# The value rows of a hybrid decoder's attention made as channel rows and then transposed

## The chip, the cores and the metric

The kernel runs on one core of one Trainium2 chip. The metric is the device time of one execution in microseconds; the median of three runs stands for a kernel. The profiler takes one execution apart into instructions. Five engines work side by side and meet only at semaphores: TensorE (PE; its weight loads are listed apart as PEld), VectorE (DVE), ScalarE (ACT), GpSimd (POOL) and SyncE (SP), which issues the large transfers.

## What is computed

One inference step of two layers for 280 token rows: 272 prompt rows (16 of them learned meta tokens) and 8 sample rows. All arrays are float32. The part that matters here is the input projection of layer 0 and the attention that uses the value rows:

```python
def mixer_inputs(h, w_in, q_norm, k_norm, pos):
    z = h @ w_in
    u, q, k, v, qi, ki, wi = jnp.split(z, SPLITS, axis=-1)
    ...
    v = v.reshape(B, L, N_HEADS, HEAD_DIM)

def sparse_attend(q, kg, vg, valid):
    ...
    p = jax.nn.softmax(logits, axis=-1)
    out = jnp.einsum('bhqk,bqkhd->bqhd', p.astype(vg.dtype), vg, ...)
```

Here `h` is the normed input (280 rows of 1024), and `v` is 280 rows of 8 heads x 64 = 512. `v` is also an output of the step. Beside it layer 0 has a state-space part (`u`, a GELU and a gate called glu), an index score that selects 64 keys for each query, and a dense feed-forward part; layer 1 has a pooling mixer and a top-2-of-8 expert part.

## The kernel before

Constants: `T = 280` token rows, split into `TC = 3` chunks of 128, 128 and 24 (`TCN`), `C = 8` input chunks of 128 channels, `H = 8` heads of `HD = 64`. Activations lie channel-major: channels on the partitions, tokens along the free axis (`h3[:, c, t]`). Weights come in as units of 2 MB (`MIXER_UNITS`: u, qi, kw, q, k, v, glu, wout0, wout1) into three slots.

**PSUM.** TensorE writes into eight banks of 128 x 512. `fill_order()` (L151) lists every fill of layer 0 up to the expert part in the order in which TensorE makes them. The seven banks of `BANKS` are dealt out by turns along that list, and a fill has to wait until the fill before it in its bank is released: `open_fill` waits for that, `filled` waits for a fill, `emptied` for its release. So the list sets both the order on TensorE and who waits for whom.

**The projections.** q, k, qi and kw are made by `channels` (L899): a block of 128 weight columns is stationary, the 280 tokens move, 8 matmuls of 128x280 for each of 4 blocks. The result is channel-major. The value rows are made the other way round, by `project` (L879): 128 (or 24) tokens of `h3` are stationary and 512 weight columns move, so that the result is token-major, as the attention needs it (`z3["v"]`, keys on the partitions).

**The order around the value rows on TensorE.** After the index dots (L1021) and the last state output come `value_rows(0)` and `value_rows(1)` (L1034, L1035), 8 matmuls of 128x512 each, then the four glu fills (L1042), which wait for the GELU (semaphore `gelu`, made by POOL at L811). Then the attention's own list: `logits(0)` and `logits(1)` (L1103, one matmul a head), `kself` (L1074), `("qB", b)` for samples 0 to 4 (L1084, L1085), `value_rows(2)` (8 matmuls with 24 tokens stationary), the transposed probabilities `pT` (L1111), `("att", 0)` (L1122), `logits(2)`, the key rows `kt` (12 transposes, L1097), `attT` (L856), qB 5 and 6, `pT` of chunk 1, qB 7, `att` 1, and so on to `satt` (L1137), the sample's attention over the cached values, and then the output projection.

**ScalarE** copies the value rows out of PSUM (`copy_rows`, recorded at L1466) between the steps of the GELU, takes the tanh of the glu fills (L1581) and makes the gate (L1583), then the exponentials (`exps`, L1591), and behind them the copies of v 2, `pT`, `kt`.

**VectorE** runs the top-64 selection (L2050, L2054) and turns it into a mask (L2059, L2060); then `mask_logits(0)` (L2066), the gate product (L2091), `mask_logits(1)`, five `key_logits(b)` (L2105 product, L2108 sum over the head, one pair for each sample), `scale_rows(0)` (L2084, which waits for `("att", 0)`), `mask_logits(2)`, `key_logits` 5 to 7 and `scale_rows(1)`.

**SP** loads the v unit into slot 2. The next unit in that slot, wout1 (L590), waits for the last fill that reads v, by `last_fill` (L145).

Of the kernel before, what the change touches and what calls it, by code (L numbers as in the profile page):

```python
# [24 lines left out]
P = 128  # L25
D = 1024
C = D // P
NP_ = 272
NB = 8
T = NP_ + NB  # L30
TC = 3
TCN = [128, 128, 24]
# [112 lines left out]
def last_fill(unit):  # L145

    if unit == "v":
        return (unit, TC - 1)
    if unit in ("u", "qi", "q", "k", "glu"):
        return (unit, 3)  # L150
    if unit.startswith("wout"):  # L151
        return ("wout", 4 * int(unit[4:]) + 3)
    if unit.startswith("ffn"):
        return ("up", 2 * int(unit[3:]) + 1)
    if unit.startswith("down"):
        return ("down", int(unit[4:]))
    return ("pool", C - 1) if unit == "pool" else unit
# [12 lines left out]
def fill_order():  # L170
# [14 lines left out]
    f += index_order()  # L185
    f += [("v", 0), ("v", 1)] + [("glu", c) for c in range(4)]
    def logits(t):
        return [("logit", t, h) for h in range(H)]
# [4 lines left out]
    def spread(*bs):  # L193
        return [("qB", b) for b in bs]

    f += logits(0) + logits(1) + ["kself"] + spread(0, 1, 2, 3, 4) + [("v", 2)] + probs_T(0) + [("att", 0)] + logits(2)
    f += [("kt", t) for t in range(TC)] + [("attT", 0)] + spread(5, 6) + probs_T(1) + spread(7) + [("att", 1)]
# [21 lines left out]
FILLS = fill_order()  # L219
FILL_NO = {name: n for n, name in enumerate(FILLS)}  # L220
SAMPLE_BANK = 7

# [4 lines left out]
def bank_of(name):  # L227
    return SAMPLE_BANK if name in SAMPLE_FILLS else FILL_NO[name] % BANKS


def bank_uses(name):

    if name in SAMPLE_FILLS:
        return SAMPLE_FILLS.index(name) + 1
    return FILL_NO[name] // BANKS + 1

# [8 lines left out]
PASS_FILL_AT = {name: k for names in PASS_FILLS for k, name in enumerate(names)}  # L245
BEFORE_FILL = [sum(bank_of(n) == b for n in FILLS) for b in range(BANKS)] + [len(SAMPLE_FILLS)]

# [45 lines left out]
def hybrid_step(nc, a, o):  # L293

    with ExitStack() as ctx:
# [116 lines left out]
        kself = qbd[:, 1408:1408 + 64]  # L412
        sqh = zk[:, 0:4 * T].rearrange("p (c t) -> p c t", c=4)
        kisT = zv[:, 0:2 * PAST].rearrange("p (r k) -> p r k", r=2)
        srelu = zv[:, 2 * PAST:2 * PAST + SK]
# [415 lines left out]
        def _(pe):  # L831
# [46 lines left out]

            def project(name, width, t, out):  # L879

                w = unit(name, width)
                for c in range(C):
                    last = mm(out[0:TCN[t], 0:width], h3[:, c, t * P:t * P + TCN[t]], w[:, c, :],  # L883
                              start=(c == 0), stop=(c == C - 1))
                return last

            def state_inputs(j):
# [140 lines left out]

            def value_rows(t):

                unit_there("v")
                project("v", 512, t, open_fill(("v", t))).then_inc(full(("v", t)), 1)

            value_rows(0)  # L1034
            value_rows(1)  # L1035
            unit_there("glu")
# [32 lines left out]
            for name in [n for n in FILLS if n[0] in PROMPT_FILLS or n in PROMPT_FILLS]:  # L1069
# [17 lines left out]
                nq = QN[t]  # L1087
                if name == ("pT", 0, 0):
                    value_rows(2)
                if name == ("att", 2):  # L1090
# [354 lines left out]
        def _(act):  # L1445
# [128 lines left out]
            A(gb, ga, ACT.Identity, scale=0.044715, bias=ones[:, 0:1]).then_inc(sem("gelu_factor"), 1)  # L1574
            copy_rows(("v", 0), z3["v"])
            act.wait_ge(sem("gelu_arg"), 1)
            A(gb, ga, ACT.Tanh, scale=GELU_C).then_inc(sem("gelu_tanh"), 1)
            copy_rows(("v", 1), z3["v"])
            for c in range(4):
# [29 lines left out]
            exps(1, 4, H)  # L1609
            copy_rows(("v", 2), z3["v"])  # L1610
            copy_probs(0, 0)
# [913 lines left out]
```

## Time and profile before

| What | us |
|---|---|
| median of three runs (1565.76, 1572.68, 1574.19) | 1572.68 |
| the profiled execution: span from its first to its last instruction | 1572.0 |
| TensorE busy | 1526.3 (97%) |
| VectorE busy | 1297.4 (83%) |
| ScalarE busy | 992.9 (63%) |
| the expert part, from about 560 to the end | some 1010 |

The profiled execution's own time is its span of 1572.0 us; it stands 0.7 us under the median of the runs, and what lies around the span is not listed apart. The page cuts the span into 40 equal slices of 39.3 us; the work of this change lies in the fifth to seventh:

```profile
PE   6998899999998999999999999999999999999998
DVE  8978883666644899899889889889989889988886
ACT  5111342544432677777787787777777778777774
PEclk9999798999999899999999999999999999999999
```

Each digit is the busy share of a slice in tenths; PEclk is the clock that TensorE was granted, in tenths of full speed.

### The profile page before, as it was taken

The page shows a single profiled execution, that of the slowest core. Times are in us where ns is not written, and L with a number is a line of the kernel's source. Part 1 is how long each engine was busy: PE and PEld are TensorE (multiplying, and loading weights), DVE is VectorE, ACT ScalarE, POOL GpSimd, SP SyncE. Part 2 cuts the span into 40 slices and gives each one's busy share as a digit, 9 for nine tenths or more (in the row PEclk, how much of TensorE's full clock was granted, in tenths as well). Part 3 has the DMA queues.
Part 4 walks back from the last instruction along what each step waited for, and adds up shares of the span by engine and source line. Part 5 has one row for each costly group of instructions (what it writes and reads, how often), then busy time and mean ns, then how long its engine had stood idle before and what let it go on. Part 6 is the DMA issues. An engine that isn't in the chain of part 4 may idle for free.

```text
span 1572.0 us, 23245 instructions
## 1 busy us (share of the span) xinstructions
PE 1526.3 (97%) x7600; PEld 1228.8 (78%) x7600; DVE 1297.4 (83%) x1721; ACT 992.9 (63%) x1304; POOL 109.1 (7%) x155
## 2 busy tenths in 40 slices
PE   6998899999998999999999999999999999999998
PEld 5665465999998678888888888888888888888886
DVE  8978883666644899899889889889989889988886
ACT  5111342544432677777787787777777778777774
POOL 1277600000000000000000000000000000000000
PEclk9999798999999899999999999999999999999999
DMA  6401144454464479999989989999999999999992
GB/s 232 161 28 54 60 164 134 154 181 161 128 180 157 155 287 367 360 318 354 383 309 358 370 317 361 365 337 330 371 346 324 371 353 316 368 372 327 347 363 86
DMA packets 212890, 420.82 MB, mean 268 GB/s; under 512 B 10233, under 2 KB 56469, under 8 KB 212572
## 3 DMA queue, kind: packets, MB, share of 16 engines
q1 hardware_dynamic: 211542, 414.37, 74.1%
q10 hardware_dynamic: 622, 3.45, 0.6%
q0 software_dynamic: 672, 2.32, 0.4%
q8 instruction: 29, 0.48, 0.1%
q14 instruction: 25, 0.20, 0.0%
HBM read 417.50 MB, written 3.07 MB: 268 GB/s over the span
## 4 chain that ended last, share of the span: by engine, by line
PE 84%; DVE 3%; issue 1%; ACT 1%; SPq 0%; DMA 0%; ACTq 0%; DVEq 0%
PE bank L1352 20%; PE bank L1351 20%; PE bank L1347 20%; PE bank L1186 3%; PE bank L1190 3%; PE bank L1189 3%; PE bank L1372 2%; PE bank L1201 1%; PE bank L1205 1%; PE bank L1204 1%; PE bank L883 1%; PE bank L1307 1%; PE bank L1387 1%; PE bank L1153 1%; PE bank L1156 1%
## 5 line engine op out<-in xcount | busy, mean ns | idle before, releaser
L2266 DVE TENSOR_TENSOR split<-raw_w,split 128x1024 fp32r<-128x1024 f32 x672 | 787.2, 1218 | 36.6 <-ACT split L1736 32.7
L1736 ACT ACTIVATE split<-raw_w 128x1024 fp32r<-128x1024 f32 x672 | 688.6, 1060 | 119.0 <-PE bank L1347 117.1
L1347 PE MATMUL bank<-split,xgr 128*128 128x512 f32 x896 | 357.5, 399 | 1.1 <-DVE xgr L2333 1.1
L1352 PE MATMUL bank<-split,xgr 128*128 128x512 f32 x896 | 353.5, 395 | 0.0
L1351 PE MATMUL bank<-split,xgr 128*128 128x512 f32 x896 | 353.3, 394 | 0.0
L1352 PEld LDWEIGHTS bank<-split,xgr 128*128 128x128 f32 x896 | 168.7, 188 | 39.5
L1347 PEld LDWEIGHTS bank<-split,xgr 128*128 128x128 f32 x896 | 168.8, 188 | 38.6 <-issue 1.3
L1351 PEld LDWEIGHTS bank<-split,xgr 128*128 128x128 f32 x896 | 168.9, 188 | 37.6
L1347 PE MATMUL bank<-split,hbr 128*128 128x512 f32 x448 | 178.0, 397 | 0.0
L1352 PE MATMUL bank<-split,hbr 128*128 128x512 f32 x448 | 176.9, 395 | 0.0
L1351 PE MATMUL bank<-split,hbr 128*128 128x512 f32 x448 | 176.8, 395 | 0.0
L1186 PE MATMUL bank<-split 128*128 128x280 f32 x352 | 102.8, 292 | 0.0
L1190 PE MATMUL bank<-split 128*128 128x280 f32 x352 | 102.5, 291 | 0.0
L1189 PE MATMUL bank<-split 128*128 128x280 f32 x352 | 102.1, 290 | 0.0
L1352 PEld LDWEIGHTS bank<-split,hbr 128*128 128x128 f32 x448 | 84.3, 188 | 19.8
L1347 PEld LDWEIGHTS bank<-split,hbr 128*128 128x128 f32 x448 | 84.3, 188 | 19.2
L1351 PEld LDWEIGHTS bank<-split,hbr 128*128 128x128 f32 x448 | 84.4, 188 | 19.1
L1685 ACT ACTIVATE split<-ring 128x1024 fp32r<-128x1024 f32 x44 | 46.6, 1059 | 65.2 <-PE bank L1186 65.2
L1818 ACT ACTIVATE late<-bank 128x512 f32<-128x512 f32 x56 | 33.5, 598 | 71.8 <-PE bank L1352 71.8
L2376 DVE TENSOR_TENSOR hbr<-bank,hbr 128x512 fp32r<-128x512 f32 x56 | 38.6, 689 | 48.4 <-ACT hbr L1795 48.2
L2176 DVE TENSOR_TENSOR split<-ring,split 128x1024 fp32r<-128x1024 f32 x44 | 53.9, 1225 | 19.2 <-ACT split L1685 19.1
L1186 PEld LDWEIGHTS bank<-split 128*128 128x128 f32 x352 | 66.3, 188 | 0.0
(433 smaller groups left out, 1976.3 us busy)
## 6 DMA issues: line engine op xcount, KB each, us to landing
raw_w<-in_moe_gate SPq DMA_DIRECT2D x112, 1024.0 KB, 5.7
raw_w<-in_moe_up SPq DMA_DIRECT2D x112, 1024.0 KB, 6.1
raw_w<-in_moe_down SPq DMA_DIRECT2D x112, 1024.0 KB, 5.9
ring<-in_w_gate SPq DMA_DIRECT2D x11, 1024.0 KB, 5.1
ring<-in_w_up SPq DMA_DIRECT2D x11, 1024.0 KB, 7.4
ring<-in_w_down SPq DMA_DIRECT2D x8, 1408.0 KB, 6.6
ring<-in_w_in SPq DMA_DIRECT2D x5, 2048.0 KB, 9.7
ring<-in_w_out SPq DMA_DIRECT2D x2, 2048.0 KB, 8.1
```

The lines of the kernel that those rows point to most:

```text
L1186: first = mm(out[:, 0:T], w[0][:, c, :], dense_in(0, c), start=(c == 0), stop=False)
L1189: mm(out[:, 0:T], w[0][:, c, :], dense_in(1, c), start=False, stop=False)
L1190: last = mm(out[:, 0:T], w[1][:, c, :], dense_in(0, c), start=False, stop=(c == C - 1))
L1347: first = mm(out, hi, place[:, s, 0, cols], start=start, stop=False)
L1351: mm(out, lo, place[:, s, 0, cols], start=False, stop=False)
L1352: last = mm(out, hi, place[:, s, 1, cols], start=False, stop=stop)
L1685: A(place[:, n % FF_PLACES, 0, :].rearrange("p (c m) -> p c m", c=C), unit(name, 256)[:, k * C:(k + 1) * C, (f % 2) * P:(f % 2) * P + P], ...
L1736: A(place[:, s, 0, :], raw_w[:, at:at + BLOCK], ACT.Copy).then_inc(sem("high_ready"), 1)
L1818: A(th[:, j % 2, :], bank[b][:, :], ACT.Silu).then_inc(bank_free[b], 1)
L2176: TT(low_, unit(f"ffn{f // 2}", 256)[:, k * C:(k + 1) * C, (f % 2) * P:(f % 2) * P + P], high.bitcast(F32), ALU.subtract).then_inc(sem("ff ...
L2266: TT(place[:, s, 1, :], raw_w[:, at:at + BLOCK], place[:, s, 0, :].bitcast(F32), ALU.subtract).then_inc(sem("low_ready"), 1)
L2376: TT(dst, src, high.bitcast(F32), ALU.subtract).then_inc(bank_free[PASS_BANK[name]], 1)
```

## The change

The value rows are now made in two steps. First `channels` makes four channel-major fills `("vc", 0..3)` out of the v unit, as it does for q and k: a block of 128 weight columns is stationary and the 280 tokens move. ScalarE copies each to `vT3`, a part of `za` that is free by then. Then TensorE transposes them into token rows, 4 blocks for each of the 3 chunks, and ScalarE copies these to `z3["v"]` as before. All three chunks are made ahead of glu; `value_rows(2)` behind qB 4 is gone. The list gets three `skip` entries, which take a number but no bank use, so that banks are now looked up in a table `FILL_AT`.

```diff
@@ def last_fill(unit):
     if unit == "v":
-        return (unit, TC - 1)
+        return ("vc", 3)
@@ def fill_order():
-    f += [("v", 0), ("v", 1)] + [("glu", c) for c in range(4)]
+    f += four("vc") + [("skip", k) for k in range(3)] + [("v", t) for t in range(TC)] + four("glu")
...
-    f += logits(0) + logits(1) + ["kself"] + spread(0, 1, 2, 3, 4) + [("v", 2)] + probs_T(0) + [("att", 0)] + logits(2)
+    f += logits(0) + logits(1) + ["kself"] + spread(0, 1, 2, 3, 4) + probs_T(0) + [("att", 0)] + logits(2)
@@
+def fill_table():
+
+    used, table = [0] * BANKS, {}
+    for n, name in enumerate(FILLS):
+        if name[0] != "skip":
+            used[n % BANKS] += 1
+            table[name] = (n % BANKS, used[n % BANKS])
+    return table
@@ hybrid_step
+        vT3 = za[:, 1, :, :]
@@ tensor
-            def project(name, width, t, out):
-
-                w = unit(name, width)
-                for c in range(C):
-                    last = mm(out[0:TCN[t], 0:width], h3[:, c, t * P:t * P + TCN[t]], w[:, c, :],
-                              start=(c == 0), stop=(c == C - 1))
-                return last
...
-            value_rows(0)
-            value_rows(1)
+            for c in range(4):
+                channels(("vc", c), "v", c * P, P)
+            for t in range(TC):
+                out = open_fill(("v", t))
+                for c in range(4):
+                    if t == 0:
+                        emptied(pe, ("vc", c))
+                    last = nc.tensor.transpose(out[0:TCN[t], c * P:(c + 1) * P], vT3[:, c, t * P:t * P + TCN[t]], ident)
+                last.then_inc(full(("v", t)), 1)
...
-                if name == ("pT", 0, 0):
-                    value_rows(2)
@@ scalar
-            copy_rows(("v", 0), z3["v"])
+            copy_channels(0)
             act.wait_ge(sem("gelu_arg"), 1)
             A(gb, ga, ACT.Tanh, scale=GELU_C).then_inc(sem("gelu_tanh"), 1)
-            copy_rows(("v", 1), z3["v"])
+            for c in range(1, 4):
+                copy_channels(c)
+            for t in range(TC):
+                copy_rows(("v", t), z3["v"])
...
             exps(1, 4, H)
-            copy_rows(("v", 2), z3["v"])
             copy_probs(0, 0)
```

On TensorE, behind the last index dots, before (L883 is `project`, L1042 the glu fills, L1103 the logits):

```order
L1021 MATMUL bank<-ring,low 16x272 x8
L883 MATMUL bank<-ring,hT 128x512 x16
L1042 MATMUL bank<-ring 128x280 x16
L1103 MATMUL bank<-low 128x128 x8
L1103 MATMUL bank<-low 128x256 x8
```

and at the same place in the changed kernel (line numbers are the changed file's: L910 is `channels`, L1042 the new transposes, L1050 glu, L1109 the logits):

```order
L1027 MATMUL bank<-ring,low 16x272 x8
L910 MATMUL bank<-hT,ring 128x280 x32
L1042 MATMUL bank<-consts,low 128x128 x8
L1042 MATMUL bank<-consts,low 24x128 x4
L1050 MATMUL bank<-ring 128x280 x16
L1109 MATMUL bank<-low 128x128 x8
L1109 MATMUL bank<-low 128x256 x8
```

The 16 matmuls of 512 columns became 32 of 280 and 12 transposes, all ahead of glu.

Further on, on TensorE, from the last qB fill (qB 4) to `("att", 0)`, before:

```order
L1084 MATMUL bank<-qsr 128x512 [waits bank1_free]
L1085 MATMUL bank<-qsr 128x512
L883 MATMUL bank<-ring,hT 24x512 [waits bank2_free,slot2_full]
L883 MATMUL bank<-ring,hT 24x512 x7
L1111 MATMUL bank<-consts,ring 128x128 [waits probs,bank3_free]
```

and now, down to the fourth logits fill of chunk 2 (L1092 and L1093 are qB 4, L1117 `pT`, L1128 `att` 0, L1109 the logits):

```order
L1092 MATMUL bank<-qsr 128x512 [waits bank2_free]
L1093 MATMUL bank<-qsr 128x512
L1117 MATMUL bank<-consts,ring 128x128 [waits probs,bank3_free]
L1117 MATMUL bank<-consts,ring 128x128 x3
L1117 MATMUL bank<-consts,ring 128x128 [waits probs,bank4_free]
L1117 MATMUL bank<-consts,ring 128x128 x3
L1128 MATMUL bank<-low,ring 128x64 [waits bank3_free,bank4_free,bank2_free,bank5_free]
L1128 MATMUL bank<-low,ring 128x64 x7
L1109 MATMUL bank<-low 16x272 [waits bank6_free]
L1109 MATMUL bank<-low 16x272 [waits bank0_free]
L1109 MATMUL bank<-low 16x272 [waits bank1_free]
L1109 MATMUL bank<-low 16x272 [waits bank2_free]
```

The 8 matmuls with 24 tokens stationary are gone. qB 4 lies in bank 2 now, the bank that the fourth logits fill of chunk 2 takes next; before, that bank held v 2, and the third logits fill took the bank of qB 4.

## Rows read from the trace of the kernel before

**Rows 1.** The page: span, and the chain that ended last by engine

```profile
span 1572.0 us, 23245 instructions
...
PE 84%; DVE 3%; issue 1%; ACT 1%; SPq 0%; DMA 0%; ACTq 0%; DVEq 0%
```

**Rows 2.** The chain in order of time, 176 to 268: start us, us, what

```profile
178.79 13.93 PE bank L883 x32
192.72 1.59 issue
194.31 7.79 PE bank L1042 x32
...
209.37 0.43 PE bank L1084
...
211.93 8.62 PE bank L883 x16
...
248.47 3.62 PE bank L1137 x4
...
263.86 1.93 PE bank L1137 x4
```

**Rows 3.** The timeline, 191 to 203: start us, us, engine, line, operation [idle before <-releaser]

```profile
191.66 2.55 POOL L811 TENSOR_TENSOR ring<-ring 128x1120 f32<-128x1120 f32 x1
...
201.71 0.43 DVE L2060 SCALAR_TENSOR_TENSOR ring<-ring,consts 40x272 f32<-40x272 f32 x1
...
202.13 0.40 ACT L1581 ACTIVATE ring<-bank 128x280 f32<-128x280 f32 x1 [1.48 <-PE bank L1042]
...
202.67 0.29 DVE L2066 CUSTOM_DVE_ANT_0 ring<-bank,ring 128x128 f32<-128x128 f32 x1 [0.53 <-PE bank L1103]
```

**Rows 4.** The timeline, 221 to 229: `scale_rows(0)` (L2084) and what follows

```profile
221.32 1.22 DVE L2108 TENSOR_REDUCE low<-low 128x16 f32<-128x1024 f32 x1
...
224.46 0.69 DVE L2084 TENSOR_TENSOR ring<-bank,small 128x512 f32<-128x512 f32 x1 [1.81 <-PE bank L1122]
...
226.22 1.53 PE L1097 MATMUL bank<-consts,low 128*128 128x128 f32 x12
...
227.59 0.60 PE L856 MATMUL bank<-consts,ring 128*128 128x128 f32 x4
...
228.88 1.22 DVE L2105 TENSOR_TENSOR low<-ring,bank 128x1024 f32<-128x1024 f32 x1 [0.49 <-PE bank L1085]
```

**Rows 5.** TensorE in stretches: window us, length, busy (x), granted clock, DMA share, GB/s

```profile
164.00:174.00 10.00, 10.00 (x37) 0.50 0.00 1
...
190.00:196.00 6.00, 4.41 (x14) 1.00 0.04 11
...
206.00:208.00 2.00, 1.40 (x11) 1.00 0.00 0
...
209.00:214.00 5.00, 5.00 (x10) 0.50 0.01 2
...
215.00:216.00 1.00, 1.00 (x3) 0.92 0.53 158
...
220.00:236.00 16.00, 14.80 (x112) 1.00 0.88 294
...
240.00:252.00 12.00, 11.68 (x61) 0.50 0.08 22
...
562.00:1572.00 1010.00, 1003.96 (x4480) 1.00 0.94 340
```

**Rows 6.** The chain, 150 to 300: four transposes (of the sample's query rows) at the half clock

```profile
169.67 0.94 PE bank L1015 x4
```

**Rows 7.** The timeline, 229 to 248: chunk 1's `pT` and `att`, chunk 2's exponentials, `att` 2

```profile
229.24 1.97 PE L1111 MATMUL bank<-consts,ring 128*128 128x128 f32 x16
...
231.85 0.51 ACT L1591 ACTIVATE ring<-ring,small 16x272 f32<-16x272 f32 x1
...
232.14 3.76 PE L1122 MATMUL bank<-low,ring 128*128 128x64 f32 x32 [0.27 <-ACT ring L1466]
...
236.13 1.34 PE L1111 MATMUL bank<-consts,ring 16*128 16x16 f32 x24 [0.24 <-ACT ring L1591]
...
237.08 0.69 DVE L2084 TENSOR_TENSOR ring<-bank,small 128x512 f32<-128x512 f32 x1
...
240.09 6.95 PE L1122 MATMUL bank<-low,ring 128*16 128x64 f32 x48
```

More of the change, by code:

```diff
@@ L220 @@
 FILL_NO = {name: n for n, name in enumerate(FILLS)}
+def fill_table():
[5 more added lines that the diff above has]
+    return table
+FILL_AT = fill_table()
 SAMPLE_BANK = 7
@@ L227, in bank_of @@
 def bank_of(name):
-    return SAMPLE_BANK if name in SAMPLE_FILLS else FILL_NO[name] % BANKS
+    return SAMPLE_BANK if name in SAMPLE_FILLS else FILL_AT[name][0]
 def bank_uses(name):
@@ L234, in bank_uses @@
         return SAMPLE_FILLS.index(name) + 1
-    return FILL_NO[name] // BANKS + 1
+    return FILL_AT[name][1]
 PASS_FILLS = [[("gate", j) for j in range(0, FC, 2)], [("up", j) for j in range(0, FC, 2)],
@@ L245 @@
 PASS_FILL_AT = {name: k for names in PASS_FILLS for k, name in enumerate(names)}
-BEFORE_FILL = [sum(bank_of(n) == b for n in FILLS) for b in range(BANKS)] + [len(SAMPLE_FILLS)]
+BEFORE_FILL = [sum(bank_of(n) == b for n in FILL_AT) for b in range(BANKS)] + [len(SAMPLE_FILLS)]
 AHEAD_FILLS = {PASS_BANK[name]: k for name, k in ((("gather", 0), 2), (("gather", 1), 2), (("y", 0), 1), (("y", 1), 1))}
@@ L1027, in _ @@
                        start=True, stop=True).then_inc(full("sscore"), 1)
-            def value_rows(t):
-                unit_there("v")
-                project("v", 512, t, open_fill(("v", t))).then_inc(full(("v", t)), 1)
-            value_rows(0)
-            value_rows(1)
+            for c in range(4):
[7 more added lines that the diff above has]
+                last.then_inc(full(("v", t)), 1)
             unit_there("glu")
@@ L1574, in _, with copy_channels @@
             A(gb, ga, ACT.Identity, scale=0.044715, bias=ones[:, 0:1]).then_inc(sem("gelu_factor"), 1)
-            copy_rows(("v", 0), z3["v"])
+            def copy_channels(c):
+                filled(act, ("vc", c))
+                copy_out(("vc", c), vT3[:, c, :], n=T)
+            copy_channels(0)
             act.wait_ge(sem("gelu_arg"), 1)
             A(gb, ga, ACT.Tanh, scale=GELU_C).then_inc(sem("gelu_tanh"), 1)
-            copy_rows(("v", 1), z3["v"])
+            for c in range(1, 4):
+                copy_channels(c)
+            for t in range(TC):
+                copy_rows(("v", t), z3["v"])
             for c in range(4):
```

## The prediction

> **What bounds the kernel.** I read the page first. TensorE holds 84% of the chain that ended last, VectorE 3% [rows 1]. Then TensorE in stretches: from 562 us to the end it is busy for 1003.96 of 1010 us at the full clock [rows 5], so nothing that happens in the mixer changes that part; it can only shift it. The question is by how much the hand-over to the output projection, near 266 us, comes earlier or later. There the chain in order of time names the value rows: 13.93 us for chunks 0 and 1, a gap of 1.59, glu for 7.79, and 8.62 for chunk 2 [rows 2]. That looks like 22.55 us of work on the path. The timeline of the other engines says that most of it is not. VectorE runs its selection until 202.14 and takes up the first logits at 202.67, with 0.53 us idle [rows 3]: TensorE and VectorE arrive there within half a microsecond of each other. And while TensorE makes the value rows of chunk 2, VectorE is in its key products and sums until 222.54 and then waits 1.81 us for `att` 0 [rows 4]. So the second piece has cover for all but 1.81 us, and the first has a partner that is just as late.
>
> **Part 1, the value rows ahead of glu.** The trace records a float32 matmul twice, so 16 matmuls of 512 columns are 32 records. Glu is 32 records with 280 columns and 128 stationary columns, in 7.79 us: 0.243 us each [rows 2]. The new fills have the same form: 4 fills x 8 matmuls x 2 records x 0.243 = 15.6 us, from 178.79 to 194.4. Bounds: by columns alone, from the 512-column record (13.93 / 32 = 0.435, x 280 / 512 = 0.238), 15.2; from above, by the 24-token matmuls, which began at the half clock (8.62 / 16 = 0.54 a record [rows 2], x 280 / 512 = 0.295), 18.9. I take glu's, the same form at the clock that holds there. Then the last block must be copied by ScalarE before its transpose: some 0.1 to hand over, 0.40 for a copy of 128x280 [rows 3], 0.1 back: 195.0. Of the 12 transposes three need only earlier copies; the other nine go at the pace of the key rows' transposes, 12 in 1.53, or 0.12 each with what follows [rows 4], 1.1 us: 196.1. Glu's other condition, the GELU, is ready at 194.21 [rows 3], so the gap of 1.59 is filled, not added. Glu ends at 203.9 instead of 202.10: **+1.8 us**, and VectorE, which had only 0.53 of its own wait there, begins the logits 1.8 later. ScalarE's extra work (4 copies of 0.40 and one more of rows) lies under TensorE's 15.6 us, except the last copy, counted above. Its wait for the fourth block stands behind the tanh of the GELU, so it holds back nobody but the glu tanh, which comes later anyway. SP's load of wout1 is released by the vc fills, ahead of the place where SP is; POOL issues its third store of value rows some 20 us sooner, and nobody waits for it until the stores are asked for behind the output projection's start.
>
> The rows give 0.12 us from one transpose to the next. The Trainium skill, page "TensorE: Matmul & The Clock Gate", Part 4 on the PE-mode transpose, gives about 275 ns for a 128x128 transpose in a kernel and so speaks against adding them. If that were the spacing, nine would take 2.5 us and this part would be +3.2 instead of +1.8; I go by the rows' spacing, since these transposes do not wait for one another.
>
> **Part 2, the value rows of chunk 2 are gone from behind qB 4.** 8.62 us less on TensorE, but VectorE's key sums now end 1.8 later, at 224.3. `att` 0 is ready by then: qB 4 ends near 213.7, 8 transposes and 16 records follow, under 6 us even at the half clock (0.235 each [rows 6]). So the 1.81 us wait goes [rows 4], and `scale_rows(0)` starts at 224.5 instead of 224.46. **-1.8 us**; parts 1 and 2 cancel, sum about 0.1. That is the whole gain of 7 us of TensorE time less 0.5 for the transposes: it falls into cover.
>
> What is late next: TensorE cannot run ahead. Its fourth logits fill of chunk 2 now takes the bank of qB 4, released when VectorE's fifth product ends, at 221.3 + 1.8 = 223.1; its last one waits for VectorE's first mask of chunk 2, after `scale_rows(0)`, as before. The key rows, `attT` 0 and qB 5 stand behind that. So they start at 226.3, where they start now [rows 4].
>
> **Part 3, the clock.** The granted clock was 1.00 in 206 to 208, 0.50 (1.2 GHz of 2.4) in 209 to 214, and 0.92 in the slice from 215, in the midst of the value rows of chunk 2, which TensorE ran without a gap; from 220 to 236 it was 1.00 [rows 5]. The change takes that steady work away and leaves idle time: after `att` 0 and three logits fills, near 220, TensorE waits until 223.1, makes four short matmuls and waits again until 226. In 206 to 208 it was busy for 1.40 of 2 us and lost the clock right after; a gap of 1.59 us in 190 to 196 did not cost it [rows 5]. I hold it likelier than not that the work from 226 on starts at the half clock, and that it comes back near 233.5 in steady work, as it did at 215. The price: 12 key transposes at 0.235 [rows 6] instead of 1.46 in all, +1.4; `attT` 0, four at 0.235, +0.5; qB 5, two records at 0.43 [rows 2] instead of half of that, +0.4; the last logits fill +0.2. VectorE's key product 5 waits for qB 5 (it waits 0.49 now [rows 4]) and starts 2.5 later, at 231.4. TensorE goes on: qB 6 until 232, then 16 `pT` transposes, six at 0.235 and ten at 0.12, until 234.7, where they end at 231.2 now [rows 7], +3.5. ScalarE's eight exponentials of chunk 2 stand behind their copies, and `pT` of chunk 2 waits for these (0.24 idle now [rows 7]): +3.5; 0.3 of it is swallowed by the wait for `scale_rows(1)` that stands behind. From there to `satt` everything is one chain, at the half clock now as then. **+3.2 us.** Bounds: 0 if the clock holds; +8 if it does not come back before `att` 1 is done.
>
> **Sum:** 1572.0 + 1.8 - 1.8 + 3.2, rounding up the 0.1 left of the first two: 1575.3 for a profiled execution, and, as that one stood 0.7 under the median of 1572.68, **1576.0** for the median.
>
> **The rivals.**
>
> *The clock holds* (0.32). For it: the gap of 1.59 us that cost nothing. Then only 0.1 is left: 1572.8.
>
> *Faster* (0.11): the clock's second low stretch, 240 to 252 [rows 5], moves. If TensorE comes back to the full clock later, near 233, it may still hold it through `att` 2 and the first sums of `satt`. `att` 2 took 6.95 us for 48 records, where 32 took 3.76 at the full clock [rows 7], so 5.6: -1.3; the first four records of `satt` took 3.62, the last four 1.93 [rows 2]: -1.7. With no loss in part 3: 1572.7 - 3.0 = 1569.7. Against it: it needs both.
>
> *Slower, by the whole stretch* (0.09): TensorE stays at the half clock from 226 through `att` 1. Then `pT` of chunk 1 costs 3.8, qB 7 0.9, and `att` 1's 32 records with 128 stationary columns some 0.235 each, 7.5 us instead of 3.76: they end near 244, and `scale_rows(1)` starts there instead of at 237.08 [rows 7], +7; `pT` of chunk 2 and the sample's logits add 1: +8, 1580.7. It decides if the clock is not back by about 236. The stretch 164 to 174, fully busy at 0.50 for 10 us [rows 5], speaks for it, as does the small size of these matmuls.
>
> My own case has 0.48.
>
> **The numbers.** About 0.5%, 7.9 us, is what a measurement of this kernel can tell from no change; the runs before lie 8.4 us apart. The cases reach from 1569.7 to 1580.7; with the scatter of the runs on both sides I give **1567 to 1582**. Only the slow rival's upper half, or scatter on top of mine, gets beyond +0.5%: 0.09. Beyond -0.5% only scatter: 0.04. Same: 0.87.
>
> **What would show it.** Right: the 64 records of the new fills from 178.8 to 194.4; VectorE's first logits near 204.5, its wait before them grown to 2.3; no wait before `scale_rows(0)`, which starts at 224.5 all the same; a granted clock of 0.50 somewhere in 224 to 233, and `satt` starting 3 us later. Wrong if VectorE's first logits start before 203 or after 206 (part 1), if `scale_rows(0)` still waits for TensorE (part 2), or if the clock is 1.00 from 224 to 236 (then *the clock holds*). A difference of more than 8 us would mean a cause that is not in this list, since from 268 on nothing of the change remains.

## The result, and the profile after

| | before | after |
|---|---|---|
| median, us (lowest to highest, runs) | 1572.76 (1565.76 to 1574.22, 7) | 1577.99 (1576.96 to 1578.69, 7) |
| ratio, with its 95% interval | | 1.0041 (1.0023 to 1.0058) |
| span of the profiled execution, us | 1572.0 | 1576.1 |

The changed kernel is slower, by 0.41%. That lies inside the forecast range of 1567 to 1582 and inside its "within 0.5%", 2.0 us above the forecast of 1576.0.

The page of the changed kernel, cut to the lines that answer to [rows 1] and to the slices shown of before:

```profile
span 1576.1 us, 23324 instructions
...
PEclk9999777999999899999999999999999999999999
...
PE 83%; DVE 4%; issue 1%; SPq 0%; ACT 0%; DMA 0%; DVEq 0%
```

The granted clock of the fifth to seventh slices reads 777 where it read 798. The rest is as it was. The chain in order of time (start us, us, what) answers to [rows 2]; L910 is now the value fills, L1472 ScalarE's copies out of PSUM, L1042 the value transposes, L1050 glu, L1103 the key rows' transposes, L1128 `att`, L1117 `pT`:

```profile
179.09 15.30 PE bank L910 x64
194.41 0.41 ACT low L1472
194.87 1.20 PE bank L1042 x9
196.07 7.55 PE bank L1050 x32
...
226.38 2.75 PE bank L1103 x12
...
233.64 4.85 PE bank L1128 x32
238.48 2.03 PE bank L1117 x24
```

The timeline (start us, us, engine, line, operation [idle before <-releaser]) at the places of [rows 3, 4, 7]; L2079 is the logits, L2097 `scale_rows`, L2118 the key product:

```profile
204.19 0.29 DVE L2079 CUSTOM_DVE_ANT_0 ring<-bank,ring 128x128 f32<-128x128 f32 x1 [1.76 <-PE bank L1109]
...
224.21 0.69 DVE L2097 TENSOR_TENSOR ring<-bank,small 128x512 f32<-128x512 f32 x1
...
230.38 1.22 DVE L2118 TENSOR_TENSOR low<-ring,bank 128x1024 f32<-128x1024 f32 x1 [2.23 <-PE bank L1093]
...
238.57 0.69 DVE L2097 TENSOR_TENSOR ring<-bank,small 128x512 f32<-128x512 f32 x1
...
243.68 6.95 PE L1128 MATMUL bank<-low,ring 128*16 128x64 f32 x48
```

And TensorE in stretches (window, length, busy (x), granted clock, DMA share, GB/s), to be held against [rows 5] (the last stretch is that of before's 240 to 252):

```profile
206.00:212.00 6.00, 4.80 (x30) 1.00 0.00 0
212.00:216.00 4.00, 2.96 (x15) 0.52 0.16 42
216.00:220.00 4.00, 3.16 (x15) 0.50 0.67 177
220.00:226.00 6.00, 4.12 (x12) 0.50 0.72 214
226.00:230.00 4.00, 4.00 (x20) 0.60 1.04 386
230.00:236.00 6.00, 5.73 (x43) 1.00 0.89 313
236.00:240.00 4.00, 4.00 (x33) 0.51 0.58 197
240.00:252.00 12.00, 11.68 (x76) 0.50 0.16 45
```

Before, the clock was low from 209 to 215 and again from 239 to 252, and 1.00 between. Now it is low from 212 to 229, full for some 7 us, and low again from 236 until after 252.

**Where the time came from.** The two profiles differ by 4.1 us: 0.3 is there when the first value matmul begins (178.79 against 179.09), before anything that the change touches. To compare kernels I take two marks in each timeline: the first record of the value fills, and the first record of the output projection, which reads `wxr` (before 178.72 and 266.71, after 179.02 and 270.12). The way between them is 87.99 us before and 91.10 after: **+3.1**. The other 0.7 us lies behind the second mark, where TensorE issues nothing that the change touches. Yet most of it belongs to the changed program and not to chance: from the first transpose of `late` in the expert part (L1397, now L1403; at 664.9 and 668.4 us) to the end of the span are 907.1 us before and 907.7 after, and the two lengths return in the traces of all the experiments below: 907.1 to 907.2 in the five traces with the old value rows (before, e2, e4, e5, b1) and 907.7 in the nine with the new ones. Its cause is open; no run was made for it.

The places of the two traces, counted from the start of the value rows in the chain (178.79 and 179.09), show where the 3.1 us arise. The first logits come at +25.10 where they came at +23.88 (1.2 later), `scale_rows(0)` at +45.12 where it came at +45.67 (0.55 earlier: its wait of 1.81 is gone), key product 5 at +51.3 where it was at +50.1 (1.2 later, behind a wait of 2.23), `scale_rows(1)` at +59.5 for +58.3 (1.2 later), `att` 2 at +64.6 for +61.3 (3.3 later). So 1.8 us is lost between `scale_rows(0)` and key product 5, in the first low stretch of the clock, and 2.1 between `scale_rows(1)` and `att` 2, where the second one now begins 3 us sooner. What glu costs (1.2) and what the wait saves (1.8) leave 0.6 of gain ahead of that.

### The profile page after: what moved, and what is told of

It is laid out like the page before. It is cut to its first block, busy times and chain, and to the rows that moved or that the text cites. A ratio compares the mean times of both kernels' runs of the same rounds, so it can differ in the third digit from the quotient of the medians.

```text
span 1576.1 us, 23324 instructions
## 1 busy us (share of the span) xinstructions
PE 1530.7 (97%) x7628; PEld 1239.7 (79%) x7628; DVE 1298.1 (82%) x1721; ACT 995.1 (63%) x1308; POOL 109.2 (7%) x155
## 4 chain that ended last, share of the span: by engine, by line
PE 83%; DVE 4%; issue 1%; SPq 0%; ACT 0%; DMA 0%; DVEq 0%
PE bank L1358 19%; PE bank L1357 19%; PE bank L1353 19%; PE bank L1192 3%; PE bank L1196 3%; PE bank L1195 3%; PE bank L1378 2%; PE bank L1207 1%; PE bank L1211 1%; PE bank L1210 1%; PE bank L1313 1%; PE bank L1393 1%; PE bank L910 1%; PE bank L1159 1%; PE bank L1162 1%
## 5 line engine op out<-in xcount | busy, mean ns | idle before, releaser
L910 PE MATMUL bank<-hT,ring 128*128 128x280 f32 (+1 forms) x272 | 73.7, 433 | 0.0
```

Source lines behind the costliest of these rows:

```text
L910: last = mm(out[0:width, 0:T], w[:, c, at:at + width], h3[:, c, :], start=(c == 0), stop=(c == C - 1))
```

## The experiments

The theory: the change gains what it takes from TensorE only where VectorE waited for it, which is about what it puts ahead of glu; the loss is the clock, because the steady work that brought it back at 215 is gone. Rivals: the loss is the order alone (all value rows ahead of the first logits), or the banks (the fills of `logits(2)` that wait for the bank of qB 4). Each ratio is to the kernel before as timed beside it (its medians there were 1572.01 for e1 to e4, 1573.02 for e5, k1 and k2, 1573.52 for k3_fill_gap and k4, 1573.71 for b1 and a1, 1572.90 for k3_again). The median of before differs between these sets by 1.7 us, so small differences are read from the ratios, not from medians of two sets. A is the first value matmul and O the first matmul of the output projection, both in us from the span's start; each comes from one profiled execution.

| kernel | median (lowest to highest, runs) | ratio to before, interval | A | O | O - A |
|---|---|---|---|---|---|
| before | 1572.76 (7) | | 178.72 | 266.71 | 87.99 |
| after | 1577.99 (7) | 1.0041 (1.0023 to 1.0058) | 179.02 | 270.12 | 91.10 |
| e1_warm | 1574.58 (1573.58 to 1575.70, 11) | 1.0013 (1.0003 to 1.0024) | 178.73 | 266.45 | 87.72 |
| e2_less_v2 | 1574.05 (1568.99 to 1575.25, 11) | 1.0010 (0.9995 to 1.0024) | 178.81 | 266.73 | 87.92 |
| e3_kt_early | 1578.35 (1572.70 to 1582.60, 6) | 1.0042 (1.0026 to 1.0058) | 171.64 | 264.50 | 92.86 |
| e4_before_kt_early | 1575.08 (1570.29 to 1576.14, 11) | 1.0012 (0.9999 to 1.0026) | 176.10 | 263.52 | 87.42 |
| e5_v2_ahead | 1580.06 (1573.57 to 1582.22, 12) | 1.0046 (1.0029 to 1.0064) | 179.56 | 275.01 | 95.45 |
| k1_spread | 1571.44 (1565.92 to 1574.25, 12) | 0.9986 (0.9969 to 1.0004) | 178.89 | 265.96 | 87.07 |
| k2_spread_warm | 1574.46 (1570.67 to 1575.22, 12) | 1.0012 (0.9998 to 1.0026) | 178.88 | 267.06 | 88.18 |
| k3_fill_gap | 1568.74 (1565.13 to 1570.74, 5) | 0.9967 (0.9954 to 0.9980) | 177.69 | 261.48 | 83.79 |
| k3_again | 1570.36 (1564.19 to 1571.85, 12) | 0.9983 (0.9970 to 0.9996) | 175.28 | 259.96 | 84.68 |
| k4_fill_two | 1570.98 (1564.33 to 1574.63, 12) | 0.9986 (0.9972 to 1.0001) | 177.83 | 265.02 | 87.19 |
| b1_before_fill | 1572.54 (1569.56 to 1573.58, 11) | 0.9996 (0.9982 to 1.0010) | 178.84 | 265.85 | 87.01 |
| a1_after_fills | 1572.45 (1567.33 to 1573.72, 11) | 0.9993 (0.9981 to 1.0006) | 177.73 | 265.16 | 87.43 |

### e1_warm: give the clock its work back

The changed kernel, with 8 matmuls behind qB 4 whose result nobody uses, of the form of the removed ones (24 stationary columns, 512 moving), into the bank that is kept for the sample:

```diff
+                if name == ("pT", 0, 0):
+                    emptied(pe, "sscore")
+                    for c in range(8):
+                        mm(ps("slogit")[0:24, 0:512], h3[:, c, 256:280], unit("glu", 512)[:, c % 4, :], start=(c == 0), stop=(c == 7))
```

> The changed kernel with 8 useless matmuls (24 tokens stationary, 512 columns moving, result never read) put where the value rows of chunk 2 used to stand, behind qB 4; nothing else differs. If the loss is the clock (removal of steady work): the granted clock is 1.00 from about 220 to 236 as before the change, the output projection starts at about 267 instead of 270.1, and the kernel is about 3 us faster than the changed one although it does 8 us more work on TensorE: within 0.1% of before. If the loss is the later glu alone, or the banks: no gain, 1577 to 1579, VectorE's first logits at 204.2 and everything behind them as in the changed kernel. If the cover for that work is gone: scale_rows(0) waits again and it is slower than the changed kernel, 1580.

The same stretches of TensorE as shown of after:

```profile
212.00:216.00 4.00, 4.00 (x7) 0.60 0.17 56
216.00:220.00 4.00, 4.00 (x10) 1.00 0.74 197
220.00:226.00 6.00, 5.17 (x42) 1.00 0.74 199
226.00:230.00 4.00, 4.00 (x31) 1.00 1.05 380
...
236.00:240.00 4.00, 3.65 (x40) 0.89 0.71 214
```

and three rows of its timeline (L1099 is the useless work, L2101 `scale_rows`, L2122 the key product, L1132 `att`):

```profile
211.51 8.74 PE L1099 MATMUL bank<-ring,hT 128*24 128x512 f32 x16
...
224.18 0.69 DVE L2101 TENSOR_TENSOR ring<-bank,small 128x512 f32<-128x512 f32 x1 [0.29 <-PE bank L1132]
...
228.61 1.22 DVE L2122 TENSOR_TENSOR low<-ring,bank 128x1024 f32<-128x1024 f32 x1 [0.49 <-PE bank L1093]
```

8.74 us of useless work on TensorE make the kernel 3.4 us **faster** than the changed one: 1574.58 against 1577.99 in the medians, all 11 runs under the lowest of the changed kernel's 7; 87.72 against 91.10 from A to O. By the ratios to before it is 0.28%, with intervals that just touch (1.0024 and 1.0023). `scale_rows(0)` stands where it stood, key product 5 is 1.8 us earlier and its wait is 0.49 again, as in [rows 4]. Orders, banks and value rows are those of the changed kernel, so neither the order alone nor the banks make these 3.4 us. What differs in the trace is the granted clock: 1.00 from 216 on where it was 0.50, and the second fall near 239 again instead of 236. It is the clock.

### e2_less_v2: take the work away and nothing else

The kernel before, where the value rows of chunk 2 get only the first of their 8 matmuls; the value rows of the last 24 tokens are therefore sums over 128 of the 1024 input channels. No order, bank or transpose changes.

```diff
-                for c in range(C):
+                n = 1 if t == 2 else C
+                for c in range(n):
```

> The kernel before with the value rows of chunk 2 cut to the first of their 8 matmuls (so 7/8 of the sum for tokens 256 to 279 is left out). The orientation, the order and the banks stay. If the clock is the cause: TensorE has 7.5 us less to do, VectorE's wait of 1.8 us before scale_rows(0) goes, yet the clock is 0.50 somewhere in 222 to 232 and the kernel is 1 to 2 us slower than before. If work on TensorE is what counts: 1.8 us faster or more, 1571. If that work was wholly hidden: no difference.

TensorE in stretches, and the timeline (L2085 is `scale_rows`, L2106 the key product):

```profile
220.00:226.00 6.00, 4.49 (x19) 0.54 0.79 234
```

```profile
222.76 0.69 DVE L2085 TENSOR_TENSOR ring<-bank,small 128x512 f32<-128x512 f32 x1
...
227.85 1.22 DVE L2106 TENSOR_TENSOR low<-ring,bank 128x1024 f32<-128x1024 f32 x1 [1.15 <-PE bank L1086]
```

Removing 7 of the 8 matmuls leaves 1.90 us of work where 8.62 stood [rows 2]. It brings `scale_rows(0)` 1.7 us forward, its wait of 1.81 [rows 4] being gone. Then 0.7 is lost before key product 5, and the second fall of the clock comes near 236 instead of 239: the output projection starts at 266.73, where it started at 266.71. The ratio says no change; the 1 to 2 us of loss that the clock theory gave are not seen, though its interval, -0.05 to +0.24%, does not exclude them. This is the second half of the change by itself: work off TensorE, wait gone, nothing gained, the clock at 0.54 where it was 1.00 [rows 5].

### e3_kt_early and e4_before_kt_early: steady work a little sooner

The 12 transposes of the key rows go ahead of `logits(2)`, so that TensorE has work while VectorE is in its key sums; e3 does so in the changed kernel, e4 in the kernel before.

```diff
-    f += logits(0) + logits(1) + ["kself"] + spread(0, 1, 2, 3, 4) + probs_T(0) + [("att", 0)] + logits(2)
-    f += [("kt", t) for t in range(TC)] + [("attT", 0)] + spread(5, 6) + probs_T(1) + spread(7) + [("att", 1)]
+    f += logits(0) + logits(1) + ["kself"] + spread(0, 1, 2, 3, 4) + probs_T(0) + [("att", 0)] + [("kt", t) for t in range(TC)] + logits(2)
+    f += [("attT", 0)] + spread(5, 6) + probs_T(1) + spread(7) + [("att", 1)]
```

> The changed kernel with the 12 key-row transposes moved ahead of the logits of chunk 2, into the time in which TensorE waits for VectorE (218 to 223). If the loss runs through key transposes, attT 0 and qB 5 at the half clock: attT 0 starts 2 us earlier, VectorE's wait before key product 5 (2.2 us) goes to about 0 and the kernel gains 2 us, 1576. If the loss is elsewhere (att 1 at the half clock): qB 5 comes earlier but the output projection starts at 270 as before.

> The kernel before the change with the same move of the 12 key-row transposes ahead of the logits of chunk 2. TensorE is at the full clock there and not idle, so the transposes push the logits of chunk 2 by 1.5 us behind att 0, and VectorE's masks wait for them; attT 0 comes no earlier. 0 to +1.5 us against before. If instead the order of the key transposes is a gain of its own: 0.5 us faster (the wait of 0.49 before key product 5).

In the changed kernel the move gains nothing: 92.86 from A to O, median 1578.35, with six runs spread over 10 us. Its profile caught an execution whose value rows began 7 us earlier, so its places are counted from A. Up to `scale_rows(0)` it stands where after stands (45.20 us behind A, 45.19 there). The wait ahead of key product 5 is 1.56 us, not about 0: the product comes 0.3 sooner, not 2, since the transposes ran at the half clock in their new place too (2.46 us). After a short return near 214 to 216 the clock was not back before 227, 56 us behind A (50 in after), so `pT` of chunk 1 ran at the half clock as well (3.67 us) and `scale_rows(1)`, which waited for nothing in after, waits 1.76. In the kernel before (e4) the timeline shows (L2084 `scale_rows(0)`, L2105 key product 5):

```profile
220.32 0.69 DVE L2084 TENSOR_TENSOR ring<-bank,small 128x512 f32<-128x512 f32 x1 [0.31 <-PE bank L1122]
...
225.41 1.22 DVE L2105 TENSOR_TENSOR low<-ring,bank 128x1024 f32<-128x1024 f32 x1
```

The wait ahead of key product 5 is gone and A to O is 0.6 shorter. But `scale_rows(0)`, which stands ahead of the moved transposes, is 1.5 us sooner behind A already, since the clock was back earlier in this execution (1.00 from 212 on); from there to key product 5 it is 5.1 us where before had 4.4. So the move itself gains nothing, and the ratio of 1.0012 agrees, with an interval that just takes in 1.

### e5_v2_ahead: the order of the change, in the old form

The kernel before with `value_rows(2)` moved ahead of glu, still with tokens stationary and without transposes.

```diff
-    f += [("v", 0), ("v", 1)] + [("glu", c) for c in range(4)]
+    f += [("v", 0), ("v", 1), ("v", 2)] + [("glu", c) for c in range(4)]
...
             value_rows(1)
+            value_rows(2)
...
-                if name == ("pT", 0, 0):
-                    value_rows(2)
```

> The kernel before with the value rows of chunk 2 moved ahead of glu in their old form (24 tokens stationary, 512 columns): the order alone, without the new orientation and without transposes. Glu is reached 6.9 us of matmuls later less the gap of 1.6, so VectorE's first logits come 5.2 us later than before (3.7 later than in the changed kernel); the 1.8 us before scale_rows(0) go; the clock falls as in the changed kernel, +3. Output projection at about 273, 6.5 us later than before: 1579 for the median, 0.4% slower than before and slower than the changed kernel. If the orientation and its transposes were the loss instead of the order and the clock: as before, 1572 to 1574.

Its chain, and its timeline (L2065 logits, L2104 key product):

```profile
179.62 20.91 PE bank L883 x48
200.53 7.74 PE bank L1043 x32
```

```profile
208.85 0.29 DVE L2065 CUSTOM_DVE_ANT_0 ring<-bank,ring 128x128 f32<-128x128 f32 x1 [5.89 <-PE bank L1102]
...
234.80 1.22 DVE L2104 TENSOR_TENSOR low<-ring,bank 128x1024 f32<-128x1024 f32 x1 [2.00 <-PE bank L1086]
```

A to O is 7.5 us longer than before, and 4.4 longer than after. The value rows take 20.91 here, and 15.30 + 0.46 + 1.20 = 16.96 in the changed kernel: the new orientation itself is worth 4 us on the path, since a matmul with 24 tokens stationary takes as long as one with 128 (48 records in 20.91, 0.436 each, as the 32 of [rows 2] alone), and one with 280 columns moving 0.239. VectorE waits 5.89 us for the first logits, 5.4 more than before, and then the clock takes its part (a wait of 2.00 ahead of key product 5, 0.49 before). So the change is a good rewrite of the value rows put in a place where all of them stand on the path.

### k1_spread and k2_spread_warm: the same form, spread over the list

If the form is good and the place is bad, the work should go where VectorE doesn't wait for it. In k1 three of the four value fills and the key rows' transposes stand ahead of glu, the fourth fill between qB 1 and qB 2, and the value transposes between qB 2 and qB 3; ScalarE's copies move with them:

```diff
-    f += [("v", 0), ("v", 1)] + [("glu", c) for c in range(4)]
+    f += [("vc", c) for c in range(3)] + [("kt", t) for t in range(TC)] + four("glu")
...
+    f += logits(0) + logits(1) + ["kself"] + spread(0, 1) + [("vc", 3)] + spread(2) + [("v", t) for t in range(TC)] + spread(3, 4)
+    f += [("skip", k) for k in range(3)] + probs_T(0) + [("att", 0)] + logits(2)
+    f += [("attT", 0)] + spread(5, 6) + probs_T(1) + spread(7) + [("att", 1)]
```

k2 adds two useless matmuls ahead of `att` 0 and two ahead of `logits(2)`.

> The new orientation, but spread: three of the four channel fills and the 12 key-row transposes ahead of glu, the fourth fill between qB 1 and qB 2, the value transposes between qB 2 and qB 3. By the clock theory TensorE is steadily busy for some 6 us more between 209 and 216, idle before 222 all the same. VectorE's first logits at 202.3 (no wait for glu), no wait before scale_rows(0), no key transposes ahead of qB 5, so no wait before key product 5. If the clock holds from 222 on: the output projection at about 264, 2.7 us before the kernel before, 1570. If it is at 0.50 there: about even with before, 1572 to 1574.

> As k1_spread, with 4 useless matmuls of 512 columns (result never read): two ahead of att 0 and two behind it, where TensorE waits for VectorE anyway. By the clock theory the granted clock is 1.00 from about 218 to 236 and the output projection starts 2 to 3 us before that of k1_spread if k1_spread lost the clock there, at about 264; median 1570 against 1572.7 of before. If idle time and not the clock is what counts, it is equal to k1_spread or up to 2 us slower.

The timeline of k1 (L2124 key product 5, L2103 `scale_rows(1)`):

```profile
226.67 1.22 DVE L2124 TENSOR_TENSOR low<-ring,bank 128x1024 f32<-128x1024 f32 x1
...
234.87 0.69 DVE L2103 TENSOR_TENSOR ring<-bank,small 128x512 f32<-128x512 f32 x1
```

Neither waits now; nor does `scale_rows(0)`, at 222.79. (Key product 2 now waits 0.58 us, behind the fourth value fill.) `scale_rows(1)` starts 2.2 us sooner than before, with the clock at 1.00 from 212 to 234. But at O only 0.75 is left of it, because the second fall of the clock has come forward too (below). The median is 6.5 us under the changed kernel's, 0.55% by the ratios; against before the interval takes in 1. The 2.7 us at O that were expected if the clock held did not come. In k2 the clock was already full where the filler went, so it could only cost: O is 1.1 later.

### k3_fill_gap, k3_again and k4_fill_two: a filler in the wait where the clock falls

In k1 TensorE waits 1.24 us for `scale_rows(1)` ahead of `attT` 1 (L871). That row, and TensorE in stretches, k1:

```profile
235.61 0.92 PE L871 MATMUL bank<-consts,ring 128*128 128x128 f32 x4 [1.24 <-DVE ring L2103]
```

```profile
234.00:236.00 2.00, 0.76 (x11) 0.97 0.87 263
236.00:238.00 2.00, 2.00 (x9) 0.50 0.58 170
```

k3 is k1 with two useless matmuls in that wait; k4 has three there and three ahead of `pT` of chunk 2.

```diff
+                if name == ("attT", 1):
+                    emptied(pe, "sscore")
+                    for c in range(2):
+                        mm(ps("slogit")[0:24, 0:512], h3[:, c, 256:280], unit("glu", 512)[:, c, :], start=(c == 0), stop=(c == 1))
```

> k1_spread, and in the gap of 1.24 us in which TensorE waits for scale_rows(1), 2 matmuls of useless work (24 stationary columns, 512 moving, 4 records, some 0.9 us at the full clock). In the profile of k1_spread TensorE was busy for 0.76 of 2 us in 234 to 236 and the granted clock fell at 236, to stay at 0.50 until about 252. If this thin stretch is what costs the clock, the filler keeps it at 1.00 past 236, the 48 records of att 2 take some 5.6 us instead of 6.95, the sample's fills ahead of them 1 us less, and the first satt matmuls 1.9 a group of four records instead of 3.6: the output projection starts 3 to 4 us earlier (262 to 263), median near 1568. If the fall was already decided by earlier idle time, or comes from the short matmuls themselves, nothing moves: output projection at 266, within 0.5 us of k1_spread.

> k1_spread with 3 useless matmuls ahead of the probabilities' transposes of chunk 2 and 3 ahead of attT 1: twelve records, some 2.6 us at the full clock, of which about 1.5 fit into TensorE's waits there. If more steady work holds the clock, it stays at 1.00 past 236 and the output projection comes 2 to 3 us earlier than in k1_spread (263 to 264). If filler cannot hold it there, it costs 1 to 1.5 us: output projection near 267, as k2_spread_warm was 1.1 later.

> The kernel of k3_fill_gap a second time, since its median rested on 5 runs. If the gain is the filler's, it shows again: median 1568 to 1570, ratio near 0.997, with the clock at 1.00 in 234 to 240 and att 2 at 4.4 us. If the first set met a lucky clock in the early part, the median falls back to that of k1_spread, near 1571.5.

The same stretches of k3_fill_gap, and then its timeline (L2107 `scale_rows`, L1109 the filler, L1137 `att` 2):

```profile
234.00:236.00 2.00, 2.00 (x9) 1.00 0.48 180
236.00:238.00 2.00, 2.00 (x22) 1.00 0.68 206
```

```profile
233.12 1.90 PE L1109 MATMUL bank<-ring,hT 128*24 128x512 f32 x4
233.69 0.69 DVE L2107 TENSOR_TENSOR ring<-bank,small 128x512 f32<-128x512 f32 x1
...
236.75 4.38 PE L1137 MATMUL bank<-low,ring 128*16 128x64 f32 x48
```

The same 48 records of `att` 2 take 4.38 us where they took 6.95 in every other kernel so far. From A to `scale_rows(1)` nothing has moved (56.0 us in both); from there to O it is 27.8 us instead of 31.1. A to O is 3.3 shorter than k1's and 4.2 shorter than before's. `attT` 1 itself starts 0.5 us later behind A than in k1. In the repeat the clock fell near 231, as the filler began; the filler ran at the half clock (3.52 us for its four records) and the clock was back behind it: `att` 2 took 4.37, and A to O 84.68, 2.4 shorter than k1's. The median of the repeat is 1.6 us above the first set's. Both intervals lie under 1, with ratios 0.33 and 0.17% below it. This is the version that beats before, by 0.2 to 0.3%, and after, by 0.6 to 0.7% as the ratios to before go. That it beats k1 is shown by the traces; the ratio of the repeat, 0.9983, is not apart from k1's 0.9986. The doubled filler of k4 held the clock too (`att` 2 in 4.38 us), but twelve records cost more than the waits they fill: 87.19, no better than k1. How much filler, and where, decides.

### b1_before_fill and a1_after_fills: the same filler in the other orders

b1 is the kernel before with the filler of k3, a1 is e1_warm with it.

> The kernel before with the filler of k3_fill_gap: 2 useless matmuls (24 stationary columns, 512 moving) ahead of attT 1, where TensorE waits only 0.35 us for scale_rows(1). They cost some 1.2 to 1.6 us there. If it is the filler that holds the clock through the sample's logits and att 2, it works here too: these take 3.6 us less (5.1 instead of 8.7 in k3_fill_gap against k1_spread), and the output projection starts 2 to 2.5 us earlier than before, at 264.3 to 264.7, median near 1570.5. If k3_fill_gap gained because its earlier part ran ahead (value rows spread), the clock falls at 239 here as before and the filler costs its 1.3 us: output projection near 268.

> e1_warm (the changed kernel with 8 useless matmuls behind qB 4) with the same 2 useless matmuls ahead of attT 1 as in k3_fill_gap. By the clock theory both low stretches are gone or late: output projection 2 to 2.5 us earlier than in e1_warm, near 264.2, median near 1572. If the filler only works in the spread order, it costs 1.3 us: output projection near 267.7, median near 1576.

The timeline of b1 (L1093 is the filler, L1126 `att` 2):

```profile
237.53 1.90 PE L1093 MATMUL bank<-ring,hT 128*24 128x512 f32 x4
239.36 0.66 PE L856 MATMUL bank<-consts,ring 128*128 128x128 f32 x4
...
241.16 4.38 PE L1126 MATMUL bank<-low,ring 128*16 128x64 f32 x48
```

In both the clock stays at 1.00 until 246, and `att` 2 takes 4.38 us: the effect does not need the spread order. But `attT` 1 starts at 239.36 where it started at 237.82 before, 1.4 later behind A, since the wait that the filler can hide in is 0.35 us here. Net, A to O is 1.0 shorter in b1, where 2 to 2.5 were expected, and the median does not move beyond its interval. In a1 it is 0.3 shorter than in e1_warm: the later part gained 1.9, and the earlier part gave most of it back, since this profile shows 0.50 in 210 to 212 where e1_warm's shows 0.95, the eight matmuls take 9.33 us instead of 8.74, and `scale_rows(0)` waits 1.86 us instead of 0.29. The medians, of two sets, differ by 2.1 us, 1572.45 and 1574.58; the ratios by 0.2%. So with two fillers the changed kernel stands where the one before stands.

What decides whether the clock holds is not shown. In before it falls at 239, although TensorE waited only 0.35 us there; in the repeat of k3 it fell as the filler began; in k3, k4, b1 and a1 it falls all the same, a few us later, near 242 to 247.

## Why the prediction came out as it did

**Part 1** (+1.8) had the right mechanism. The 64 records took 15.30 us, not 15.6, the copy with its hand-overs 0.46, not 0.6, and glu took 7.55, not 7.79; the sum came to +1.2. The spacing of the transposes nearly held: nine in 1.20 us (0.133 each, 0.12 in the forecast), though one lasts 0.273. The Trainium skill, page "TensorE: Matmul & The Clock Gate", Part 4 on the PE-mode transpose, gives about 275 ns for one of bf16 in a kernel; this trace has that duration for float32 too, but not as the price of each in a row, as the prediction's alternative of +3.2 read it. The prediction's "less 0.5 for the transposes" is a slip, since twelve at 0.12 are 1.4 us; it enters no sum.

**Part 2** (-1.8) was right. `scale_rows(0)` doesn't wait any more, and starts at 224.21 where 224.5 was forecast. e2 shows the wait go by itself.

**Part 3** (+3.2, the clock) was right in kind and nearly right in its sum, and not in its shape. The forecast had a half clock from 226 to 233.5. It lasted from 212 to 229, since it did not come back after the first fall as it had at 215, and it came back some 4.5 us sooner than I had it. Of the terms, the 12 key transposes came as forecast (2.75 us instead of 1.46); `attT` 0 and qB 5 had the full clock for the most part. So key product 5 was only 1.2 later, not 2.5. What filled the sum up is what the text gave to the slower rival in part: the second fall came at 236 instead of 239, so `att` 1 took 4.85 us instead of 3.76, and `pT` of chunk 2 2.03 instead of 1.34 [rows 7]. The start of `att` 2 was 3.3 later, where +3.2 was forecast. A sum that comes out to 0.1 us while its terms are off by a microsecond each is partly luck.

**The clock holds** (0.32) is refuted by the windows of after, and by e1. **Faster** (0.11): the second low stretch did move, but forward. Its price for `att` 2 was too low: at the full clock it takes 4.38 us, not 5.6. k3 is this rival made true by a filler, and it gains 3.3 us. **Slower** (0.09) happened over a part of `att` 1.

**The level.** From A to O +3.3 was forecast and +3.1 measured, yet the medians differ by 5.2. The step that failed is the one from the profile to the median: it takes what one profiled execution loses for what the median loses. First its level was misread. The text took the profiled execution as 0.7 under its median by holding a span against a run's time. In all 13 other kernels' profiled executions the time of the run is 2.0 to 2.2 us more than the span (after 1578.14 and 1576.1, e1_warm 1574.48 and 1572.4). So before's profile belongs, by estimate, to an execution of some 1574.1, 1.3 **above** the median, while after's lies 0.15 above its own. This slip alone did not move the forecast, which adds the same 3.3 to the median either way. The miss of 2.0 us is made up of these 1.2 between the places of the two profiled executions, 0.7 behind O, of which 0.55 came with the changed program (the prediction had "nothing of the change" there), 0.3 ahead of A, and -0.2 from A to O. Part of the 1.2 is which executions were met: two of before's seven runs lie under 1569, none of after's, and without these two the medians differ by 3.8.

## What to carry to other kernels

Before work is taken off an engine whose clock was seen to fall and rise with its activity, read the granted clock of the stretches behind it. Where that engine is not the one waited for, its idle time buys nothing (e2) and may halve the speed of what comes next; here steady work in its waits was worth more than removing it, where the clock was low or about to fall (e1, k3), and cost 1.1 us where it was full already (k2). And a rewrite that is better by itself may show little of it: the new orientation is 4 us cheaper than the old one in the same place (e5), but with the clock held it puts the kernel only 0.3 us ahead of before (e1: 87.72 against 87.99 from A to O), since most of the saved work had cover. Spread over places where nobody waits it was 0.9 ahead (k1).

## What the runs showed of the hardware that I had not expected

Useless work paid: from A to O 8 matmuls bought 3.4 us in e1, and 2 bought 3.3 in k3 (2.4 in the repeat), 1.0 in b1 and 0.3 in a1. The price depends on the wait around it: 4 records in a wait of 1.24 us put off what stood behind them by 0.5 us, in a wait of 0.35 us by 1.4. The Trainium skill, page "TensorE: Matmul & The Clock Gate", Part 1 on oscillation, tells, for matmuls with few rows that wait for DMA, to restructure the loop so that TensorE stays warm; k1, which spreads the work, agrees for the first stretch (1.00 from 212 to 234) and shows that it isn't enough for the second.

The clock in the early part of the program differs from one execution to the next, and also between two of the same kernel: it was 0.93 in 80 to 100 us in k3_fill_gap and 1.00 in k3_again, and A lies 2.4 us apart. TensorE in stretches, in the profile of after and then in that of e3_kt_early, long before the first line that either change touches:

```profile
80.00:100.00 20.00, 18.16 (x67) 0.93 0.16 53
```

```profile
80.00:100.00 20.00, 18.16 (x75) 1.00 0.15 54
```

In the second the value rows begin 7.4 us earlier (171.64 against 179.02). That is as wide as the scatter of the runs of before (8.5 us), and so likely its source. The runs' own mean clocks agree: of the 29 runs of before beside k1, those of 1565.5 to 1566.7 us have 0.982 to 0.983, those above 1574.4 have 0.976. Why the early clock differs was not followed up. This scatter is why the table compares A to O, and why one profile of a kernel says less about its median than it seems.
